# Bias tables of two attentions: read back from 128 stored copies instead of reversed by matrix products

## The reference, cut to what matters

```python
s_own = jnp.einsum('bhqd,bhjd->bhqj', qc, ko) * scale
s_own = s_own + bias_ht[:, rel_bucket(dist_own)][None]      # MOBA, dist = q - k
s_own = jnp.where(dist_own >= 0, s_own, -jnp.inf)
...
bias = bias_tab[rel_bucket(dist)].transpose(2, 0, 1)        # SWA, 0 <= dist < 128
s = jnp.where(mask[None, :, None, None], s + bias, -jnp.inf)
```

## Time and profile before

| | us |
|---|---|
| median of 3 runs | 1266.48 |
| the runs | 1263.81, 1266.48, 1266.81 |
| the profiled execution's own time | 1263.68 |
| its span in the profile | 1262.4 |
| busy: PE, DVE, ACT, POOL | 1211.1, 695.0, 591.9, 468.4 |
| mean granted clock of TensorE | 0.983 |

### The profile page before, as it was taken

The page is one execution under the profiler, slowest core; times in us unless marked ns, Lnnn a source line. Parts: engine busy times, 40 slices in busy tenths (PEclk is TensorE's granted clock), DMA queues, the critical chain, the costliest instruction groups (busy, mean ns, idle before and its releaser), DMA issues.

```text
span 1262.4 us, 19797 instructions
## 1 busy us (share of the span) xinstructions
PE 1211.1 (96%) x8329; PEld 1108.1 (88%) x8329; DVE 695.0 (55%) x980; ACT 591.9 (47%) x900; POOL 468.4 (37%) x255
## 2 busy tenths in 40 slices
PE   7999999999999999999999999999999769999998
PEld 6998888798978999988989879999889768999986
DVE  5754544357766744433789856434326696633423
ACT  6543344454454554433743345444435674544432
POOL 4342233223331354442465422444433340544441
PEclk9899989999999999999999999999999979999999
DMA  7664355344444575655544354665654433656560
GB/s 233 181 186 117 101 170 162 87 134 134 124 137 141 169 213 170 200 193 174 155 132 139 129 167 143 209 185 183 200 186 154 145 134 117 202 183 186 182 200 34
DMA packets 156578, 201.60 MB, mean 160 GB/s; under 512 B 13391, under 2 KB 131321, under 8 KB 156490
## 3 DMA queue, kind: packets, MB, share of 16 engines
q1 hardware_dynamic: 154650, 193.69, 49.6%
q0 software_dynamic: 1840, 6.64, 1.5%
HBM read 199.24 MB, written 1.07 MB: 159 GB/s over the span
## 4 chain that ended last, share of the span: by engine, by line
PE 78%; DVE 12%; ACT 6%; issue 2%; POOL 1%; DMA 0%; SPq 0%; ACTq 0%; DVEq 0%; POOLq 0%
PE bank L475 15%; PE bank L478 15%; PE bank L481 15%; PE bank L492 9%; PE bank L498 9%; PE bank L495 9%; ACT whi L947 2%; DVE wlo L1352 2%; DVE sm L1655 1%; PE bank L846 1%; DVE Ss L1786 1%; DVE ring L1657 1%; DVE uc L1482 1%; DVE qT L1780 1%; DVE ring L1643 1%
## 5 line engine op out<-in xcount | busy, mean ns | idle before, releaser
L1926 POOL TENSOR_TENSOR wlo<-raw,whi 128x1024 fp32r<-128x1024 f32 (+1 forms) x161 | 410.1, 2549 | 570.3 <-ACT whi L947 570.3
L947 ACT ACTIVATE whi<-raw 128x1024 fp32r<-128x1024 f32 x368 | 364.9, 1041 | 121.4 <-PE bank L498 115.7
L1352 DVE TENSOR_TENSOR wlo<-raw,whi 128x1024 fp32r<-128x1024 f32 x207 | 280.0, 1362 | 255.8 <-ACT whi L947 254.9
L475 PE MATMUL bank<-hh,whi 128*128 128x256 f32 x1792 | 293.9, 286 | 1.7 <-ACT hh L979 1.7
L478 PE MATMUL bank<-hh,wlo 128*128 128x256 f32 x1792 | 289.4, 284 | 1.3 <-DVE wlo L1352 0.7
L481 PE MATMUL bank<-hl,whi 128*128 128x256 f32 x1792 | 288.8, 284 | 0.0
L475 PEld LDWEIGHTS bank<-hh,whi 128*128 128x128 f32 x1792 | 248.8, 193 | 10.8 <-issue 9.7
L478 PEld LDWEIGHTS bank<-hh,wlo 128*128 128x128 f32 x1792 | 248.5, 193 | 1.8 <-DVE wlo L1352 0.9
L481 PEld LDWEIGHTS bank<-hl,whi 128*128 128x128 f32 x1792 | 248.1, 193 | 0.0
L492 PE MATMUL bank<-whi,gh 128*128 128x512 f32 x264 | 83.4, 397 | 0.0
L498 PE MATMUL bank<-whi,gl 128*128 128x512 f32 x264 | 83.1, 395 | 0.0
(11 more groups left out here) (307 smaller groups left out, 1363.0 us busy)
## 6 DMA issues: line engine op xcount, KB each, us to landing
raw<-in_ffn_w_in SPq DMA_DIRECT2D x88, 512.0 KB, 3.6
raw<-in_w_in SPq DMA_DIRECT2D x72, 512.0 KB, 3.7
raw<-in_ffn_w_out SPq DMA_DIRECT2D x44, 512.0 KB, 3.4
raw<-in_hgrn_w_in SPq DMA_DIRECT2D x32, 512.0 KB, 3.8
raw<-in_w_ffn_gate SPq DMA_DIRECT2D x22, 512.0 KB, 4.1
raw<-in_w_ffn_up SPq DMA_DIRECT2D x22, 512.0 KB, 4.1
raw<-in_w_ffn_down SPq DMA_DIRECT2D x22, 512.0 KB, 3.4
raw<-in_w_branch SPq DMA_DIRECT2D x16, 512.0 KB, 4.1
```

Source lines behind the costliest of these rows:

```text
L475: T.matmul(out, wh[:, i, c], xh[:, k, :], start=first and (i, k) == pairs[0], stop=False)
L947: A.activation(half_of(whi, j, h), half_of(raw, j, h), ACT.Copy).then_inc(s_hi[j % NS][h], 1)
L1352: V.tensor_tensor(half_of(wlo, j, h), half_of(raw, j, h), half_of(whi, j, h).bitcast(f32), ALU.subtract).then_inc(s_lo[j % NS][h], 1)
L1926: G.tensor_tensor(half_of(wlo, j, 1), half_of(raw, j, 1), half_of(whi, j, 1).bitcast(f32), ALU.subtract).then_inc(s_lo[j % NS][1], 1)
```

## The change

- `flip`, its constant, the eight products, their eight copies and `FOX_REST` are gone.
- `u_scratch` holds 128 equal copies of each head's row. POOL stores them with one DMA, in which each of the 16 rows of 1,536 bytes is the source 128 times: 2,048 rows, 3.15 MB, where there were 16 rows, 24 KB.
- Each of the two loads starts, for partition p, in copy p, at offset 127 - p: a step of 383 elements from partition to partition. It still has 1,024 rows of 1 KB.
- Units move between FOX's steps: one or two a step, none behind step 9.
- DVE waits for `s_w` at the first bias of MOBA, where PE waited for it before `win`.

```diff
-        CONST = {k: i + 1 for i, k in enumerate(["ident", "ones", "flip", "half", "pad", "tri0", "tri1", "trf", "wfox", "negu"])}
+        CONST = {k: i + 1 for i, k in enumerate(["ident", "ones", "half", "pad", "tri0", "tri1", "trf", "wfox", "negu"])}
...
-        FOX = [[("gate", 1, 0)], [("gate", 1, 1), ("ym",)], [("gate", 1, 2)], [("gate", 1, 3)], [("b", 0), ("b", 1)], [("b", 2)],
-               [("b", 3), ("bv",)], [("br", 0, 0)], [("br", 0, 1), ("win", 0)], [("win", 1), ("win", 2)]]
-        FOX_REST = [("win", c) for c in range(3, 8)]
+        FOX = [[("gate", 1, 0)], [("gate", 1, 1), ("ym",)], [("gate", 1, 2)], [("gate", 1, 3)], [("b", 0)], [("b", 1)],
+               [("b", 2), ("b", 3)], [("bv",)], [("br", 0, 0)], [("br", 0, 1)]]
...
-                else:
-                    c = what[1]
-                    b = turn(("win", c), next_bank())
-                    tq.wait_ge(s_w, 32)
-                    tq.wait_ge(*const("flip"))
-                    tq.wait_ge(*free(("win", c)))
-                    T.matmul(banks[b][:, :], flip[:, :], windows_of(c), start=True, stop=True).then_inc(s_full[b], 1)
...
-                else:
-                    aq.wait_ge(*full(*what))
-                    A.activation(windows_of(what[1]), bank_of(*what)[:, :], ACT.Copy).then_inc(evacuated(*what), 1)
...
                     if n == 1:
                         vq.wait_ge(*const("wfox"))
+                    else:
+                        vq.wait_ge(s_w, 32)
...
-            diagonal(flip, -127, 1).then_inc(s_const, 1)
...
-            G.dma_start(a["u_scratch"], rb[0:16, 16:400]).then_inc(s_u, 16)
+            G.dma_start(a["u_scratch"], rb[0:16, 16:400].rearrange("h (o n) -> h o n", o=1).broadcast_to([16, 128, 384])).then_inc(s_u, 16)
...
                     for i, dst in enumerate((wmoba, wswa)):
-                        src = bass.AP(a["u_scratch"].tensor, 8 * i * 384, [[1, 128], [384, 8], [1, 256]])
+
+                        src = bass.AP(a["u_scratch"].tensor, 8 * i * 128 * 384 + 127, [[383, 128], [128 * 384, 8], [1, 256]])
                         G.dma_start(dst, src).then_inc(s_w, 16)
...
-    args["u_scratch"] = nc.dram_tensor("u_scratch", (16, 384), f32, kind="Internal").ap()
+    args["u_scratch"] = nc.dram_tensor("u_scratch", (16, 128, 384), f32, kind="Internal").ap()
```

More of the change, by code:

```diff
@@ L92, in build @@
         ident = sbuf(root, "ident", [128, 128])
-        flip = sbuf(root, "flip", [128, 128])
         vec = sbuf(root, "vec", [128, 128])
@@ L409, in totals @@
             return fT[:, 2 * j:2 * j + 2, :].rearrange("p k t -> p (k t)") if m == 1 else tot[:, j, TOT[m]:TOT[m] + 512 // m]
-        def windows_of(c):
-            return area[:, 3072 + 512 * c:3584 + 512 * c]
         def hi_set(j, h):
@@ L749, in fill, with attention @@
                         tok.then_inc(s_full[b], 1)
-                else:
-                    c = what[1]
-                    b = turn(("win", c), next_bank())
-                    tq.wait_ge(s_w, 32)
-                    tq.wait_ge(*const("flip"))
-                    tq.wait_ge(*free(("win", c)))
-                    T.matmul(banks[b][:, :], flip[:, :], windows_of(c), start=True, stop=True).then_inc(s_full[b], 1)
-            def attention(n, fills, rest, inputs):
+            def attention(n, fills, inputs):
                 q, k, v, heads_k, window, slot = ATT[n]
@@ L803, in attention @@
                         values(i - 2)
[L804 to L810, removed]
+            attention(1, FOX, [("col", "c", j) for j in range(4)] + [("tok", "cv", t) for t in range(2)])
+            attention(2, MOBA, [("col", "b", j) for j in range(4)] + [("tok", "bv", t) for t in range(2)])
+            attention(3, SWA, [("col", "d", 0), ("col", "d", 1), ("col", "dk"), ("dv",)])
             branch(3, 0)
@@ L1114, in fill, with attention @@
                         A.activation(bh[:, 0, 2 * c:2 * c + 2, :], two(bank_of("ym", c)[:, :]), ACT.Copy).then_inc(s_bt, 1)
-                else:
-                    aq.wait_ge(*full(*what))
-                    A.activation(windows_of(what[1]), bank_of(*what)[:, :], ACT.Copy).then_inc(evacuated(*what), 1)
-            def attention(n, fills, rest):
+            def attention(n, fills):
                 slot = ATT[n][5]
@@ L1163, in attention @@
                         values_out(i - 2)
[L1164 to L1169, removed]
+            attention(1, FOX)
+            attention(2, MOBA)
+            attention(3, SWA)
             branch(3, 0)
@@ L1624, in fill, with attention @@
                                         ALU.subtract).then_inc(evacuated("ym", c), 1)
-                elif what[0] != "win":
+                else:
                     use(what)
-            def attention(n, fills, rest):
+            def attention(n, fills):
                 window, slot = ATT[n][4:]
@@ L1992, in fill @@
                     for i, dst in enumerate((wmoba, wswa)):
-                        src = bass.AP(a["u_scratch"].tensor, 8 * i * 384, [[1, 128], [384, 8], [1, 256]])
+                        src = bass.AP(a["u_scratch"].tensor, 8 * i * 128 * 384 + 127, [[383, 128], [128 * 384, 8], [1, 256]])
                         G.dma_start(dst, src).then_inc(s_w, 16)
-                elif what[0] != "win":
+                else:
                     use(what)
-            for fills in (*FOX, FOX_REST, *MOBA, *SWA):
+            for fills in (*FOX, *MOBA, *SWA):
                 for what in fills:
```

## The result

The changed kernel takes 1278.24 us (median of 4 runs, 1272.80 to 1282.25) where the kernel before, beside it, takes 1265.14. The ratio is 1.0103 with a 95% interval of 1.0071 to 1.0135: slower by 1%, where 1258.3 and a gain were forecast. The profiled execution took 1282.25 us, its span is 1281.0.

The account below looks back on a forecast made before the run. PE, busy 96% of the span, was taken to bound the kernel. The median 1266.48 less 8.22 us for removed products, with 0 for fills, moved wait and store, gave 1258.3 us, range 1254.5 to 1266.0.

Parts of the forecast that it names:

- the 0 for the added store: Early weight loading: the 3.15 MB store issued at 24.54 on POOL would cost PE 0 us.
- Removed: PE's `win` products, copies and the wait for the last copied window, all on the path: 8.22 us gained.
- FOX's fills and DVE's wait: Units moved between FOX's steps, and the window wait moved to DVE at MOBA's first bias: cost 0 each.
- Issue on POOL: POOL's issue of the store's 2,048 rows takes some 1.8 us, hidden in 4.94 us of idle time.
- How long the store takes: Store's DMA time, bounded between 9.0 us on all 16 engines and 31.8 us; the low end was taken.
- the low end: Store of 9.0 us, from queue 0's rate between 161 and 173 us; 0.14 us a packet.
- The rule I had set against it: Trainium skill: partitions 0 to 15 lie behind 4 of 16 ports, 104 GB/s; store 30.2 us, sum 4 us smaller.
- When it begins: Store's first packets at about 28.5 us, when dtf's last piece is in and z's first unit under way.
- How it shares: Each weight packet waits for one store packet; 1,024 store packets, 64 an engine, 0.14 to 0.50 us each.
- a store of 25.5 us: Longest store for which z's second unit is still in by 52.0 and PE loses nothing; 0.40 us a packet.
- Rival B: Store starts before dtf's second half passes; PE loses some 18 us waiting for dtf: 1276 us, chance 0.08.
- Rival C: PE's granted clock takes part back: one more half-speed stretch costs 3.4 us, 1261.7 us; chance 0.10.

Follow-up runs that it names:

- e2: The kernel before with only the 128-copy store from 16 partitions added, products and fills as they were, windows read from copy 0: 1286.29 us, ratio 1.0147.
- e1: The changed kernel with the store cut back to one copy (24 KB), bias tables reversed, so it measures time alone: 1257.04 us, ratio 0.9922.
- e3: The changed kernel with each head's row made on 8 partitions, so the same 2,048 rows leave from 128 partitions: 1257.15 us, ratio 0.9920.
- e4: The changed kernel with POOL waiting for the landing of dtf's second half before issuing the store: 1269.26 us, ratio 1.0029.
- e5: The changed kernel with the store's 2,048 rows leaving from partitions 0 to 31: 1260.78 us in a single run.
- e6: The changed kernel with the store's 2,048 rows leaving from partitions 0 to 63: 1263.62 us in a single run.
- e7: The changed kernel with the store leaving from 16 partitions eight apart (0, 8, ..., 120): 1267.80 us in a single run.
- e9: The changed kernel with its 16-partition store cut into eight DMAs of 16 copies, issued between POOL's weight splits: 1259.11 us, ratio 0.9949.

## Why the prediction was wrong, point by point

The step that failed is the 0 for the added store. It was built on a store of 9.0 us that begins at 28.5 and shares one for one with the weights. Measured were 31.9 us, a begin at 26.3, and 15 us in which the weights got one packet through; PE waited 17.6 us for dtf, and the store alone cost 21.5 us (e2), which turned a gain of 8 into a loss of 13.

- **Removed (8.22 us): right.** 7.9 us on PE's timeline, 7.7 in the medians of e1.
- **FOX's fills and DVE's wait (0): right.** e1 has no new wait in FOX, and the windows had landed at 174.5, long before MOBA's first bias at about 243.
- **Issue on POOL (1.8 us, hidden): right** in that it is hidden; it took 1.04 us.
- **How long the store takes: the choice failed.** The truth lay at the upper of the bounds of 9.0 and 31.8 us (31.9 measured), but I took the low one. It came from window loads, which write all 128 partitions, where this store reads 16; from 128 partitions the store does take 9.7 (e3). That "the low end comes from the same queue" compared the issuing side and not the side that limits. The rule I had set against it was right. The Trainium skill, SBUF — State Buffer, section on the DMA port swizzle, has 104 GB/s for partitions 0 to 15, and the same bandwidth for 0 to 63 as for 0 to 31. The traces agree: 103 GB/s from 0 to 15, and 19.4 us from 0 to 63 where 0 to 31 take 18.3. (What the prediction calls a sum 4 us smaller by this rule is the gain; the time would be 4 us longer.)
- **When it begins (28.5 us): wrong.** The first packet started at 26.29, 1.75 us after the issue; 2,048 rows did not cost time in proportion to the 1,024 of the window load. That put it ahead of dtf's last piece and made rival B the case that came. A later begin would have been no rescue: e4's store was issued at 28.4, and PE lost 12 us.
- **How it shares (one for one from the start): half right.** One for one holds later (315 to 318), but first some 20 packets an engine go ahead of any weight packet (7 to 22 in the other runs). The size of a packet was off as well: 43 an engine of three rows and 0.68 us, not 64 of two rows and at most 0.50. So even the reckoning by which nothing is lost up to a store of 25.5 us was too kind; e5, e6 and e7 wait 1.6 to 3.0 us with stores of 15.7 to 17.3.
- **Rival B, priced 1276 with 0.08: this is what happened,** at 1278.24: the store was ahead of dtf, and dtf landed with the store's end. That its wait of 18 us came so near the 17.6 measured is luck in part. It had 64 dtf packets an engine still to come, one for each packet of the store. Only its last piece still was, 512 rows, 32 an engine. One for one from 26.3 they would have been through at an estimated 26.3 + 32 x 0.68 = 48.1, and PE would have waited some 7 us; the head start, which B did not have, made up the rest. It also left out that the clock falls during the wait: another 4.0 us at dtf and z. The chance was too low because two conditions were weighed as if each were unlikely; the Trainium skill's figure made the first one likely, and the second rested on a single row about another transfer.
- **Rival C:** a stretch more at half clock did come in the profiled executions of the changed kernel (4 us at 390 to 402) and of e1 (3.8), beside the loss and not in place of it.

## What to carry to other kernels

In these runs the side with few neighbouring partitions set a transfer's rate: before pricing one by another of the same queue, compare how many partitions, and which, each reads and writes. A long slow transfer on one queue here kept the other queue's packets out, first wholly and then to one for each of its own slow ones, so the weight stream pays; spread it over the partitions (e3) or cut it into short pieces (e9). And where a cost has bounds far apart, look first for what would decide between them, before the cheap end is taken.

## What the runs showed of the hardware

- Reading 16 neighbouring partitions gives 103 GB/s, 128 give 370 (e3, 31 to 34 us); 0 to 63 are no faster than 0 to 31 (19.4 and 18.3 us), and 16 partitions eight apart are as fast as 64 neighbours (19.4).
- The store sent packets ahead before the weight queue got its next one through: 21 an engine in the changed kernel (15 us at 0.68 us a packet), 22 in e7, 17 in e4 in the 12.5 us shown, 14 in e3, 7 in e6. What sets the number was not tried; one fixed number does not fit.
- SP's issue of a load of dtf took 4.04 us instead of 1.27, and the next four 4.1 to 9.5 instead of mostly 0.37, while the store had the engines.
- Rows of 1,536 bytes were packed three to a packet of 4.6 KB.
- After an idle stretch of 17.6 us the granted clock was 0.53 over the next 15 us of work (60 to 75 us), so that the wait cost 4.0 us on top of its length.
